# A two-layer decoder trunk: who writes the second copy of the memory-attention queries in layer 1

## The reference, cut to what matters

```
h = x @ b_w_in[j];  u, v, qm = split(h)
mk, mv = split(mem @ w_mem_kv[i])              # 256 memory rows, 4 heads of 64
s = einsum('bshd,bmhd->bhsm', qm, mk) * 64 ** -0.5
mo = einsum('bhsm,bmhd->bshd', softmax(s), mv)
y = concat([mix, mo]) @ w_out[i]
x = layer_norm(DN_ALPHA * x + y)
```

## Time and profile before

| what | value |
|---|---|
| median of three executions | 2283.04 us |
| the profiled execution | 2282.71 us |
| its span | 2281.0 us |
| TensorE busy | 2232.3 us (98%) |
| VectorE busy | 1251.5 us (55%) |
| ScalarE busy | 863.3 us (38%) |
| GpSimd busy | 1132.8 us (50%) |
| mean granted clock of TensorE | 0.996 |

### The profile page before, as it was taken

How to read it: one execution, slowest core, us unless ns; L and a number is a source line. 1 busy time by engine, 2 the same in 40 slices (tenths; PEclk the granted TensorE clock), 3 DMA queues, 4 the chain that set the end, 5 groups by cost and what they waited for, 6 DMA issues and landing times.

```text
span 2281.0 us, 32371 instructions
## 1 busy us (share of the span) xinstructions
PE 2232.3 (98%) x11304; PEld 1889.9 (83%) x11304; DVE 1251.5 (55%) x2361; ACT 863.3 (38%) x1622; POOL 1132.8 (50%) x681
## 2 busy tenths in 40 slices
PE   8999999999999999999999999999999999999997
PEld 7888888788888888888888889988888888888886
DVE  5656556657544444545546646667535444545446
ACT  5656666613432323233214743204332323232313
POOL 4222122663765555555553593443865555555543
PEclk9999999999999999999999999999999999999999
DMA  4111111041011111111131121221011111111121
GB/s 168 56 47 38 45 41 46 30 152 52 1 56 55 55 55 55 55 46 46 47 102 47 56 54 49 75 56 37 1 56 55 55 55 55 55 55 55 38 74 74
DMA packets 161548, 128.23 MB, mean 56 GB/s; under 512 B 11568, under 2 KB 147376, under 8 KB 161456
## 3 DMA queue, kind: packets, MB, share of 16 engines
q1 hardware_dynamic: 148992, 115.36, 16.5%
q10 hardware_dynamic: 12464, 11.63, 1.6%
HBM read 122.78 MB, written 4.19 MB: 56 GB/s over the span
## 4 chain that ended last, share of the span: by engine, by line
PE 89%; DVE 6%; ACT 2%; issue 2%; DMA 1%; POOL 0%; SPq 0%; DVEq 0%; ACTq 0%
PE ps L292 26%; PE ps L294 26%; PE ps L293 26%; PE ps L639 2%; PE ps L667 1%; PE ps L626 1%; PE ps L668 1%; PE ps L627 1%; DVE XTl L1080 1%; PE ps L1419 1%; DVE XR L1011 1%; DVE st L1098 1%; DMA raw<-in_a_w_in 1%; DVE V L1949 0%; PE ps L1041 0%
## 5 line engine op out<-in xcount | busy, mean ns | idle before, releaser
L1696 DVE TENSOR_TENSOR XR<-XR,ps 128x512 f32<-128x512 f32 x576 | 378.5, 683 | 184.6 <-PE ps L294 184.6
L282 POOL TENSOR_TENSOR Wh<-raw,zcol 128x1024 fp32r<-128x1024 f32 x79 | 151.0, 1912 | 509.9 <-PE ps L294 466.0
L1619 POOL TENSOR_TENSOR Rl<-raw,Rh 128x512 fp32r<-128x512 f32 x216 | 279.2, 1293 | 199.7 <-ACT Rh L1550 199.7
L292 PE MATMUL ps<-XTh,Wh 128*128 128x512 f32 x608 | 250.1, 411 | 2.5 <-DVE XTl L1080 0.9
L292 PE MATMUL ps<-Wdh,hidh 128*128 128x512 f32 x640 | 249.2, 389 | 1.3 <-DVE XR L1696 1.3
L293 PE MATMUL ps<-Wdl,hidh 128*128 128x512 f32 x640 | 249.0, 389 | 0.0
L294 PE MATMUL ps<-Wdh,hidl 128*128 128x512 f32 x640 | 249.0, 389 | 0.0
L294 PE MATMUL ps<-XTh,Wl 128*128 128x512 f32 x608 | 239.1, 393 | 0.0
L293 PE MATMUL ps<-XTl,Wh 128*128 128x512 f32 x608 | 238.7, 393 | 0.0
L1550 ACT ACTIVATE Rh<-raw 128x512 fp32r<-128x512 f32 x216 | 135.2, 626 | 257.4 <-PE ps L294 254.4
L293 PE MATMUL ps<-XTl,Rh 128*128 128x512 f32 x576 | 224.1, 389 | 0.0
(11 more groups left out here) (231 smaller groups left out, 4948.6 us busy)
## 6 DMA issues: line engine op xcount, KB each, us to landing
raw<-in_w_gate SPq DMA_DIRECT2D x44, 512.0 KB, 4.6
raw<-in_w_up SPq DMA_DIRECT2D x44, 512.0 KB, 3.9
rawd<-in_w_down SPq DMA_DIRECT2D x36, 512.0 KB, 3.5
raw<-in_a_w_in SPq DMA_DIRECT2D x20, 512.0 KB, 3.8
raw<-in_w_out SPq DMA_DIRECT2D x16, 512.0 KB, 3.5
raw<-in_b_w_in SPq DMA_DIRECT2D x15, 512.0 KB, 3.8
B<-in_c_bias SPq DMA_DIRECT2D x12, 512.0 KB, 3.5
raw<-in_w_mem_kv SPq DMA_DIRECT2D x8, 512.0 KB, 3.8
```

The lines of the kernel that those rows point to most:

```text
L282: nc.gpsimd.tensor_tensor(high, raw[:, turn, :], zcol[:, 0:1].to_broadcast([P, UNIT]), ALU.add).then_inc(high_done, 1)
L292: nc.tensor.matmul(dst, wh, xh, start=first, stop=False, skip_group_check=onto)
L1619: nc.gpsimd.tensor_tensor(Rl[(w - 1) % 4][:, :], source(w), Rh[(w - 1) % 4][:, :].bitcast(F32), ALU.subtract).then_inc(gs[L]("low"), 1)
L1696: nc.vector.tensor_tensor(x, x, bank(4 + n % 4), ALU.add).then_inc(gf[L]("added"), 1)
```

## The change

For the pairs of layer 1 (`g >= 8`) ScalarE no longer makes the second copies of the high parts. VectorE makes them, each right behind the low part of the same head. The semaphore and its counts stay as they are. Layer 0 is not changed.

```diff
@@ q_act
         for hd in range(2):
             nc.scalar.activation(bf.Qh[own(hd), hd, cs], b[own(hd), :], ACT.Copy, scale=QSCALE).then_inc(at_("q_high"), 1)
-        for hd in range(2):
+        for hd in range(0 if g >= 8 else 2):
             act.wait_ge(*at_("q_high", 2 * rank(g, "q", h) + hd + 1))
             nc.scalar.activation(bf.Qh[other(hd), hd, cs], bf.Qh[own(hd), hd, cs].bitcast(F32),
                                  ACT.Copy).then_inc(at_("q_again"), 1)
@@ q_dve
             nc.vector.scalar_tensor_tensor(bf.Ql[hd][own(hd), cs], bank(proj_bank(g, "q", h))[own(hd), :], QSCALE,
                                            bf.Qh[own(hd), hd, cs].bitcast(F32), ALU.mult,
                                            ALU.subtract).then_inc(at_("q_low"), 1)
+            if g >= 8:
+                nc.vector.tensor_copy(bf.Qh[other(hd), hd, cs], bf.Qh[own(hd), hd, cs].bitcast(F32)
+                                      ).then_inc(at_("q_again"), 1)
```

## The result

The changed kernel takes 2287.9 us (median of 17 executions, 2286.02 to 2289.32) against 2281.97 us for the kernel before (17 executions, 2280.65 to 2284.37). The ratio is 1.0023, 95% interval 1.0017 to 1.003: slower by 5.2 us (3.9 to 6.8); the two medians by themselves are 5.9 us apart. Forecast were 2292.0 us, that is +9.0 us, from 2284.0 to 2295.0 us. The direction came out, and so did the mechanism, but for the place (9, 0) in part; the size is 0.6 of what I wrote.

What follows compares the result with a forecast made beforehand. ScalarE and VectorE latency was taken to bound layer 1's query stage, not TensorE's work. 0.9 + 1.3 + 2.7 + 3.2 = 8.1 us, plus 0.9 for the clock: 2283.04 + 9.0 = 2292.0 us, range 2284.0 to 2295.0.

Steps and rivals of the forecast that it cites:

- The bound, the counts, the copy's own time: Layer 1 query stage: ScalarE and VectorE latency sets the pace; ScalarE loses eight 622 ns copies, VectorE gains eight of 0.45 us.
- That a one-source copy within SBUF waits for GpSimd: Layer 1's VectorE copies: copy and GpSimd instruction shut each other out, whoever comes second waiting until the first ends.
- Rival 1: All four layer 1 groups: the copy does not contend with GpSimd; +0.9 to +2.4 us, 2284 to 2285.5 us; chance 0.21.
- (8, 0): +0.9: First layer 1 query group: GpSimd idle, two copies of 0.45 us delay the first scores; +0.9 us.
- (8, 1): +1.3: Second layer 1 query group: copies wait for GpSimd, ending 3.2 us behind the low parts; row maximum late, +1.3 us.
- (9, 0): +2.7: Third layer 1 query group: copy pair ends 3.8 us later, TensorE's transposes have 0.67 us to spare; +2.7 us.
- an extra for the clock: New TensorE waits at (9, 0) and (9, 1) may lower its clock again; 0.9 us added, bounds 0 and 3.
- (9, 1): +3.2: Fourth layer 1 query group: copy pair ends 3.7 us later, TensorE has nothing to spare; +3.2 us.
- the sign I had named: Profile after: copies long, but scores behind (9, 0) and (9, 1) not 2.5 to 3.5 us late; mechanism right, cover larger.
- Rival 3: Layer 1's last two groups: contention mostly hidden or half as long, 1 to 1.5 us each; +4 to +5.5 us; chance 0.12.
- Rival 2: Behind (8, 1): ScalarE's freed time wins, not slower, rather faster; -0.6 us, 2282.4 us; chance 0.05.

Runs made afterwards that it cites:

- the PSUM version: The changed kernel, but VectorE makes all eight second copies from PSUM times the scale, not from SBUF: 2284.2 us against 2282.78 before, ratio 1.0006.
- the run with GpSimd's work cut: The changed kernel with GpSimd's gain and shift in layer 0's last norm done on 32 of 1024 columns only: 2285.82 us, one execution.
- the run with (9, 1) alone: Against the kernel before, VectorE makes the second copies from SBUF for group (9, 1) only: 2286.23 us against 2281.49, ratio 1.0015.
- +0.96 alone: Against the kernel before, VectorE makes the second copies from SBUF for group (8, 1) only: 2283.28 us against 2281.49, ratio 1.0006.
- the run with (8, 0) alone: Against the kernel before, VectorE makes the second copies from SBUF for group (8, 0) only: 2282.22 us against 2281.49, ratio 1.0.
- the second profile of the changed kernel: The changed kernel, with nothing altered, profiled once more: 2287.11 us, one execution, beside 2282.75 us for the kernel before.
- the run of (9, 0) alone: Against the kernel before, VectorE makes the second copies from SBUF for group (9, 0) only: 2284.98 us against 2281.49, ratio 1.0012.
- the PSUM version at (8, 1): Against the kernel before, VectorE makes the second copies from PSUM for group (8, 1) only: 2282.19 us against 2282.78, ratio 0.9997.

## Why the prediction was right or wrong, point by point

**The bound, the counts, the copy's own time.** The copies take 0.42 us undisturbed (0.45 taken). ScalarE's share in the end, 622 ns each, is gone and brought nothing at (8, 0), as written.

**That a one-source copy within SBUF waits for GpSimd.** Right, shown by three runs: the PSUM version has no wait, the run with GpSimd's work cut has none where GpSimd is gone, and the run with (9, 1) alone has the longest where the phase is worst. The rule of the Trainium skill, SBUF — State Buffer, section "Who interferes with whom", holds here for the direction that the trace before did not show. The reverse, GpSimd held up by the copy, is smaller than my 0.3 us: 2.44 us for 2.40, 2.07 for 1.89. The 0.24 us that I had read at 1392 us was no clean evidence for it either: beside that GpSimd instruction stood a second one of VectorE, with two inputs in SBUF (L1949, from 1393.02 us), which I had not weighed. Rival 1 is out.

**(8, 0): +0.9.** Measured +0.93. TensorE starts at 1276.70 us in place of 1275.42, of which 0.42 us is the start of the stage itself, and the wait is the copy's:

```profile
1276.70 0.39 PE L626 MATMUL ps<-bK,bQh 128*128 128x256 f32 x1 [1.24 <-DVE bQh L830]
```

**(8, 1): +1.3.** Measured +1.18 in the changed kernel, +0.96 alone. The copies' ends came as worked out, shifted with the stage; the pair cost 2.8 us over the low parts, not 3.2, since GpSimd was hardly later (I had added 0.3 us) and the waiting copy ended 0.28 us behind it, not 0.45. Of the 1.18 us, 0.89 stand ahead of the scores for which TensorE waited last here (at 1298.22 us, 8.29 us behind the first low part; before, at 1295.98 us, 7.40 us behind it), and 0.29 behind them, where TensorE ran at its lower clock.

**(9, 0): +2.7. This step failed.** Measured +1.20, and the reason is not the one I gave. I had let TensorE's transposes wait for the exponentials of 1301.73 us, with 0.67 us to spare. What they were late for did not matter: in this stretch of the first profile TensorE waited for VectorE not at all. All its waits, after and before alike, are one line (waits of TensorE between the low parts of (9, 0) and of (9, 1), kernel after):

```profile
PE ps L292 <- ACT V L595: 0.2, 1, 0.2
```

The pair ended 3.2 us late, not 3.8, and VectorE was 3.1 us late at the first row maximum (5.66 us less the 2.53 that the stage was late already). Of these some 2.5 us were spare, from the row maximum of 1299.79 + 0.42 us to the scores at 1302.77 us. The rest was covered by TensorE running slow. The row maximum and those scores, before:

```profile
1299.79 0.42 DVE L871 CUSTOM_DVE_ANT_0 Pm<-ps,zcol 128x256 f32<-128x256 f32 x1
...
1302.77 0.28 PE L626 MATMUL ps<-bK,bQh 128*128 128x256 f32 x1
```

And after:

```profile
1305.45 0.42 DVE L874 CUSTOM_DVE_ANT_0 Pm<-ps,zcol 128x256 f32<-128x256 f32 x1
...
1306.24 0.28 PE L626 MATMUL ps<-bK,bQh 128*128 128x256 f32 x1
```

The window of the slow stretch in the kernel before (stretch, its length, busy us of PE, PEld, DVE, ACT, POOL, granted clock, DMA share, GB/s):

```profile
1297.00:1301.00 4.00, 4.00 (x17) 3.53 (x16) 2.40 (x9) 3.83 (x9) 3.92 (x2) 0.57 0.47 135
```

The windows of the kernel after, for its slow stretch and what follows:

```profile
1298.00:1304.40 6.40, 6.18 (x23) 5.60 (x24) 4.61 (x13) 3.36 (x9) 6.32 (x4) 0.50 0.36 100
1304.40:1318.70 14.30, 14.11 (x98) 12.65 (x97) 9.27 (x37) 9.21 (x27) 14.06 (x7) 1.00 0.11 31
```

Behind the waits at (8, 1), three of 3.5 us in all in place of two of 2.9, the clock stayed at 1.2 GHz until 1304.4 us, where it had been back at 2.4 GHz by 1301 us. (1 - 0.50) x 6.4 = 3.2 us lost against (1 - 0.57) x 4.0 = 1.7 us: 1.5 us more. The instructions say nearly the same: from the last waited-for scores of (8, 1) to the scores at 1306.24 us TensorE took 8.02 us, before 6.79 us, and 5.18 us in the run with (8, 0) alone, where the clock stayed up. That is 1.23 us more at the lower clock, 0.29 of them ahead of the (9, 0) stretch and 0.94 of its 1.20 us. So in this profile what I had put at 0.9 us as an extra for the clock is most of the price of (9, 0), and it takes the place of the 2.7 us instead of standing on top.

In the second profile of the changed kernel the place cost 1.97 us, and a part of it is a wait of the kind that I had forecast. The first copy was 0.7 us longer there, the slow stretch ended at about 1301.5 us, and TensorE waited for the row maximum:

```profile
1305.14 0.39 PE L626 MATMUL ps<-bK,bQh 128*128 128x256 f32 x1 [0.87 <-DVE mneg L874]
```

With the clock up, as in the run of (9, 0) alone, the copies' lateness shows as a wait of 1.72 us and the clock falls behind it. How the price is shared between wait and clock is thus a matter of the single execution.

**(9, 1): +3.2.** Measured +1.67. The mechanism is right, the size is the phase's. I had carried 2.7 us of lateness from (9, 0) to here; with 1.2 the first copy met the last 0.2 us of a GpSimd instruction and took 0.49 us, where my average wait of 1.2 us with the copy's own 0.45 us gives 1.65. The second, bound to the whole of the next, took 1.74. The pair ended 2.3 us late, not 3.7. The low parts of the probabilities behind it (`PTl`) no longer waited for `PTh` and started 5.41 us later than before, of which the stage was late already by 3.73: 1.7 us are left. Before and after:

```profile
1317.46 0.69 DVE L879 TENSOR_TENSOR PTl<-ps,PTh 128x512 fp32r<-128x512 f32 x1 [0.44 <-ACT PTh L777]
...
1322.87 0.69 DVE L882 TENSOR_TENSOR PTl<-ps,PTh 128x512 fp32r<-128x512 f32 x1
```

With no lateness from the places ahead this place costs 3.54 us.

**The sum.** 0.93 + 1.18 + 1.20 + 1.67 = 4.98 us, against 8.1 + 0.9. TensorE's waits for the row maximum grew to 6.5 us, with 1.1 us for the copies beside them, not to 10 or more:

```profile
PE ps L626 <- DVE mneg L874: 6.5, 6, 2.5
...
PE ps L626 <- DVE bQh L830: 1.1, 1, 1.1
```

That is the sign I had named for a cover larger than worked out. The 2287.9 us lie under the forecast's own range (2288.5 to 2295.5 us) and inside the stated one only because that takes in the rivals. Rival 3, +4 to +5.5 us, has the right number, and half its reason: at (9, 1) a copy did meet a short rest of a GpSimd instruction. I gave it 0.12, and should have given it more: for the first copies of (9, 0) and (9, 1), whose phase hung on a sum of earlier estimates, I had taken the mean wait or a little more both times. Rival 2 is answered by the PSUM version at (8, 1): the gain there is 0.5 us.

**Left open.** Why the clock drops in one execution of a kernel and not in another was not settled, nor what parts the executions of one kernel into groups some 2 us apart; nor was it tried whether a copy that starts first holds GpSimd up for longer than 0.2 us at another size.

## What to carry to other kernels

Before work is moved to VectorE, look at GpSimd in the same stretch and at where the operands lie: a one-source copy within SBUF is the cheapest instruction by itself (0.42 us) and the dearest beside a GpSimd that never rests (up to 2.4 us), and the same data read from PSUM (0.69 us) is the better choice. Such a price hangs on the phase of the other engine's stream, so prices of single places don't add up: in the traces 8.7 us one by one, 5.0 and 5.7 us together. And before a late engine is charged to the path, ask at which clock TensorE runs there; its slow stretches are a cost and a cover at once.

## What was not expected of the hardware

A copy that waits ends 0.27 to 0.29 us behind the GpSimd instruction, less than the 0.42 us that it takes alone, as if 0.14 us of it could be spent while it waits. The GpSimd instruction that comes next is longer by 0.01 to 0.19 us only. And a wait of TensorE in this stage mostly costs twice: behind the waits at (8, 1), of 0.9 to 1.4 us each, ten of the twelve profiles show 3.4 to 7.0 us at 1.2 GHz (twice (1 - granted clock) x length, summed over the two middle stretches of the table), and two of them none. In the run of (9, 0) alone a part of its 6.6 us stands behind the wait of 1.72 us there.
